# Two groups of block one's input projections taken in 512-column products, with their halves copied out by ScalarE and added by GpSimd

## The reference, cut to what matters

```
h = rmsnorm(x, mix_pre_norm[l])
u = h @ w_in[l]
u_z, u_xbc, u_dt, u_ly, u_lx, u_g = jnp.split(u, list(IN_SPLITS), axis=-1)
y_a = ssd_mixer(u_z, u_xbc, u_dt, ...)
y_b = rglru_mixer(u_ly, u_lx, ...)            # gate = gelu(u_ly); return h * gate
g = jax.nn.sigmoid(u_g.reshape(b, s, N_BRANCHES, D_MODEL) + gate_b[l])
merged = g[:, :, 0, :] * (y_a @ w_proj_ssm[l]) + g[:, :, 1, :] * (y_b @ w_proj_lru[l])
x = x + rmsnorm(merged @ w_out[l], mix_post_norm[l])
```

## Time and profile before

| | |
|---|---|
| time before, median of 3 runs | 838.07 us (837.78 to 838.09) |
| the profiled execution's own time | 837.62 us |
| its span, first to last instruction | 835.8 us |
| PE busy | 825.4 us (99% of the span) |
| DVE busy | 638.2 us (76%) |
| ACT busy | 502.9 us (60%) |
| POOL busy | 74.0 us (9%) |
| mean granted TensorE clock | 0.998 |

### The profile page before, as it was taken

One profiled execution on the slowest core, in us unless ns is written; L12 is line 12 of the kernel. 1 busy time (PEld: TensorE's weight loads), 2 busy tenths in 40 slices (PEclk: granted clock), 3 DMA queues, 4 the chain that ended last, 5 costly groups with the idle time before them and its releaser, 6 DMA issues. The chain is left out here.

```text
span 835.8 us, 14603 instructions
## 1 busy us (share of the span) xinstructions
PE 825.4 (99%) x5782; PEld 741.8 (89%) x5782; DVE 638.2 (76%) x1146; ACT 502.9 (60%) x828; POOL 74.0 (9%) x71
## 2 busy tenths in 40 slices
PE   8999999999999999999999999999999999999996
PEld 6999999999989988888888789899899888888885
DVE  6887987998968778788878869777664566776765
ACT  6575778665267755556566878853544454555453
POOL 0200001101020111111111200040000020001000
PEclk9999999999999999999999999999999999999999
DMA  8657443467464746554655465574333333465541
GB/s 306 235 180 285 155 150 106 150 215 284 138 220 152 250 155 209 193 184 171 208 194 189 137 213 194 144 258 155 123 106 126 136 117 103 151 206 182 191 151 51
DMA packets 42812, 147.81 MB, mean 177 GB/s; under 512 B 6876, under 2 KB 7672, under 8 KB 42232
## 3 DMA queue, kind: packets, MB, share of 16 engines
q1 hardware_dynamic: 42600, 146.75, 52.5%
q10 hardware_dynamic: 144, 0.13, 0.0%
HBM read 145.79 MB, written 1.08 MB: 176 GB/s over the span
## 5 line engine op out<-in xcount | busy, mean ns | idle before, releaser
L2042 DVE TENSOR_TENSOR t_wl<-t_raw,t_wh 128x1024 fp32r<-128x1024 f32 x256 | 312.1, 1229 | 78.8 <-ACT t_wh L1464 77.9
L1464 ACT ACTIVATE t_wh<-t_raw 128x1024 fp32r<-128x1024 f32 x256 | 268.0, 1055 | 92.1 <-PE bank L674 89.7
L674 PE MATMUL bank<-t_hx,t_wh 128*128 128x256 f32 (+1 forms) x1968 | 298.5, 302 | 0.3 <-ACT t_hx L1475 0.3
L674 PEld LDWEIGHTS bank<-t_hx,t_wh 128*128 128x128 f32 x1968 | 263.6, 191 | 13.3 <-issue 1.1
L674 PE MATMUL bank<-t_hx,t_wl 128*128 128x256 f32 x1136 | 160.1, 283 | 0.0
L674 PEld LDWEIGHTS bank<-t_hx,t_wl 128*128 128x128 f32 x1136 | 149.2, 191 | 3.0
L674 PE MATMUL bank<-t_wh,t_hx 128*128 128x512 f32 x440 | 122.3, 400 | 0.0
L674 PE MATMUL bank<-t_wh,t_br 128*128 128x512 f32 x384 | 103.9, 392 | 0.0
L674 PEld LDWEIGHTS bank<-t_wh,t_hx 128*128 128x128 f32 x440 | 80.8, 188 | 17.5 <-ACT t_wh L1464 0.9
L674 PEld LDWEIGHTS bank<-t_wh,t_br 128*128 128x128 f32 x384 | 70.9, 188 | 14.1 <-issue 0.2
L674 PE MATMUL bank<-t_wl,t_hx 128*128 128x512 f32 x220 | 67.7, 390 | 0.0
(11 more groups left out here) (152 smaller groups left out, 685.4 us busy)
## 6 DMA issues: line engine op xcount, KB each, us to landing
t_raw<-in_ws SPq DMA_DIRECT2D x258, 512.0 KB, 4.2
t_br<-decay SPq DMA_DIRECT2D x1, 2048.0 KB, 8.8
t_arena<-in_post SPq DMA_DIRECT2D x3, 512.0 KB, 5.1
t_x<-in_xin SPq DMA_DIRECT2D x2, 512.0 KB, 4.5
t_bd<-in_bd SPq DMA_DIRECT2D x1, 1024.0 KB, 6.3
t_x<-in_xtok SPq DMA_DIRECT2D x1, 1024.0 KB, 6.5
t_arena<-in_mem SPq DMA_DIRECT2D x1, 1024.0 KB, 8.6
out<-t_x SPq DMA_DIRECT2D x3, 256.0 KB, 2.3
```

What stands on the lines that cost most here:

```text
L674: return e.matmul(o, l, r, start=st, stop=sp, skip_group_check=True)
L1464: e.activation(high(q), RAW[q % NR][:, :], ACT.Copy, bias=0.0, scale=1.0).then_inc(*hi.now(q))
L2042: e.tensor_tensor(low(q), RAW[q % NR][:, :], high(q).bitcast(F), SUB).then_inc(*lo.now(q))
```

## The change

`ly0` to `ly3` and `g4` to `g7` go through `chunk_apart`. Each of their 16 units gets a PSUM bank of its own (banks 0 to 2 in turn; before, one bank per chunk). After each unit ACT copies the bank's 512 columns to a half of `PX` (`PARTS`), which is double-buffered by the unit's place in the chunk, and POOL adds the two parts (128x256) into `LY` or `GG`. For `g4` to `g7` ACT then applies Tanh in place on `GG`, once POOL's second addition of the chunk is done. DVE's program is the same, instruction for instruction.

```diff
+BESIDE = [f"ly{i}" for i in range(4)] + [f"g{i}" for i in range(4, 8)]
...
+        elif name in BESIDE:
+            for i in range(2):
+                n = (n + 1) % 3
+                bank[name, i] = n
...
+        PARTS = [PX[:, 512 * i:512 * i + 512].rearrange("p (w t) -> p w t", w=2) for i in range(2)]
...
+        g_both = tally("parts_added")
...
+                if name[0] in BESIDE:
+                    return a_ev.of("beside", *name)
...
             for i in range(4):
-                chunk(f"ly{i}", Hh, Hl)
+                chunk_apart(f"ly{i}")
             for i in range(4, 8):
-                chunk(f"g{i}", Hh, Hl)
+                chunk_apart(f"g{i}")
...
-                    e.wait_ge(*a_ev.of(f"ly{q}"))
+                    e.wait_ge(*g_both.of(f"ly{q}", 1))
...
+            def parts_out(name):
+                for j in range(2):
+                    q = walk.unit()
+                    e.wait_ge(*unit.of(q))
+                    n = BESIDE.index(name)
+                    if n > 0:
+                        e.wait_ge(*g_both.of(BESIDE[n - 1], j))
+                    act(PARTS[j], two(BANK[name, j]), ACT.Copy).then_inc(*a_ev.now("beside", name, j))
+                    walk.tick()
...
             def gates(i):
-                walk.cols(f"g{i}", i == 0)
-                chunk_done(f"g{i}")
+                name = f"g{i}"
+                if name in BESIDE:
+                    parts_out(name)
+                    e.wait_ge(*g_both.of(name, 1))
+                else:
+                    walk.cols(name, i == 0)
+                    chunk_done(name)
...
-                    m = act(GG[:, k, :], half(BANK[f"g{i}"], j), ACT.Tanh, bias=hgb[:, k:k + 1], scale=0.5)
+                    src = GG[:, k, :] if name in BESIDE else half(BANK[name], j)
+                    m = act(GG[:, k, :], src, ACT.Tanh, bias=hgb[:, k:k + 1], scale=0.5)
...
             for i in range(4):
-                walk.cols(f"ly{i}")
-                chunk_done(f"ly{i}")
-                act(LY[:, 2 * i:2 * i + 2, :], two(BANK[f"ly{i}"]), ACT.Copy).then_inc(*a_ev.now(f"ly{i}"))
+                parts_out(f"ly{i}")
...
+            def added(name, dst, k):
+                for j in range(2):
+                    walk.unit()
+                    e.wait_ge(*a_ev.of("beside", name, j))
+                    tt(dst[:, k + j, :], PARTS[j][:, 0, :], PARTS[j][:, 1, :], ADD).then_inc(*g_both.now(name, j))
+                    walk.tick()
...
             for i in range(4):
-                walk.cols(f"ly{i}")
+                added(f"ly{i}", LY, 2 * i)
...
             for i in range(4, 8):
-                walk.cols(f"g{i}")
+                added(f"g{i}", GG, 2 * i)
```

## The result

The changed kernel takes 849.88 us (median of 4 runs, 849.46 to 850.55); the kernel before, on the same chip, 838.08 (837.78 to 838.31). The ratio is 1.0143, 95% interval 1.0131 to 1.0155: slower by 11.8 us, where 7.8 were forecast. The profiled execution took 849.46 us, against 837.62 before.

The account below looks back on a forecast made before the run. PE, 99% busy, bounds the kernel, with DVE's queue level with it up to `YBl(3)`; +1.0 and +6.9 there make PE 7.8 us later: 837.62 + 7.8 = 845.4, forecast 845.9 as median, range 841.0 to 850.5 (8 in 10).

Parts of the forecast that it names:

- C: Rival: ACT also becomes a bound, its waits for POOL delaying splits and copies; 2 to 4 us more, 849; 0.25 with D.
- D: Rival: the clock falls while PE waits in unit 52, 1.5 or 2.5 us lost, 848; 0.25 with C, the smaller part.
- the chain on DVE ends level with PE's: From 143.5 to 183.8 us DVE's queue has no slack; PE has 0.1 us to spare at `YBl(3)`, so DVE's delay is the kernel's.
- Term 1: Unit 37's copy ahead of ACT's Exp delays the split of unit 41, so DVE's queue starts 1.0 us later.
- Term 2: POOL's 13 additions of units 38 to 50 each lengthen DVE's queue by 0.53 us: +6.9 us (0 to 9.4).
- The upper bound, the whole 0.72 us: The most one POOL addition could cost DVE: the whole length of such an operation on POOL, 0.72 us.
- PE's 1.3 us: Sixteen units at 2.80 instead of 2.88 us save PE 1.3 us, forecast to be lost in its wait for DVE.
- The other waits of PE: Earlier bank reuse costed at nothing; waits at low weights and `y_pair`s lie inside the delay at `pl0`.
- the four multiplies: POOL's multiplies, only spread: three stood in DVE's way before, at 1.1 us each, and three will afterwards; no term.
- Rival A: Half of POOL's additions cost DVE nothing, falling while it waits for something else; 842.5 us; chance 0.17.
- Rival B: Neither term delays DVE at `YBl(3)`, so PE's faster products show their 1.3 us; 836.8 us; chance 0.06.
- the stages behind: Sign to look for in the profile after: the stages behind the changed stretch each take as long as before.

Follow-up runs that it names:

- e3: The changed kernel with 24 and 9 useless products on PE ahead of its waits for `YBl(2)` and `YBl(3)`; 845.82 us, ratio 1.0095.
- e1: The changed kernel with POOL's 16 additions replaced by zero fills that read nothing, sums left out; 840.47 us, ratio 1.0040.
- e5: The changed kernel with POOL's additions cut to 128x128, the other half of each sum set to zero; 845.78 us, ratio 1.0098.
- e4: The changed kernel with ACT's copy of unit 37 moved behind the Exp and the square root; 849.57 us, ratio 1.0139.
- e2: The kernel before plus only sixteen 128x256 additions of zeros on POOL, into a buffer nobody reads; 846.18 us, ratio 1.0097.
- e6: The changed kernel's 512-column products alone: ACT takes only the high halves, no POOL additions, low parts' share left out; 838.13 us, ratio 1.0000.
- e9: The kernel of e6 with the recurrence's four 128x512 multiplies on DVE instead of POOL; 837.71 us, ratio 0.9997.
- e7: The changed kernel's products, with DVE reducing each bank's two parts out of PSUM, no ACT copies or POOL additions; 852.13 us, ratio 1.0162.
- e8: The change made for g4 to g7 only, ly0 to ly3 as in the kernel before; 845.80 us, ratio 1.0089.

## Why the forecast was right, and by what it fell short

The direction, and a time within 841.0 to 850.5, were forecast; the main sum, 845.9, was not met. By my own bands, 849.88 us lies above 847.8, where I had put 0.25 for C and D, and C, to which I gave the larger part, did not happen. D brought it there, at a price that I had put too low. The range held with 0.6 us to spare, because it had room for C as well as for D, and that part is luck. DVE's delay came out at 7.9 us for 7.8, by the mechanism of the sum.

**That the chain on DVE ends level with PE's, so that its delay is the kernel's.** Right. `YBl(3)` ended at 191.70 for 191.7 forecast, released PE there, and nothing was given back behind. Where the clock was kept up (e3), the kernel took 845.82 us for 845.9.

**Term 1, the copy of unit 37 ahead of the Exp, +1.0.** Right: 144.54 for 143.53, with the executions in step ahead of it. Counted from unit 40's split it is 7.17 us for 6.19, and 7.17 again in e1, e3 and e5, which keep ACT's order. e4 adds what I hadn't seen: most of the microsecond isn't free to be won back, since POOL then works beside DVE and not ahead of it.

**Term 2, 13 x 0.53 = 6.9.** The sum is right, in part by luck, by two small errors that cancel: it was fourteen additions at 0.49, because with DVE so late unit 51's came ahead of `YBl(3)`, and because one of them fell on a gating that reads PSUM. In e2, where four did, the mean was 0.41. That turns are the cause stands on e1 (POOL writes only: gone), e2 (additions alone: there) and e5 (half the size: half the turn). The upper bound, the whole 0.72 us, is out as a mean.

**PE's 1.3 us, lost in the wait.** Right: PE's units were 2.80 us apart wherever it didn't wait (starts at 171.34, 174.14, 176.93), and it stood the longer at `YBl(2)`. Whether they would be lost without the additions as well isn't shown: e6 and e9 were no faster than the kernel before, but with 0.99 and 0.61 us of bank waits of their own in the way, and with a scatter of nearly the size in question. What the gain would be in a kernel with both obstacles removed stays open.

**The other waits of PE, at nothing, and the four multiplies, no term.** Right in sum: PE waited 1.94 us for a low split and 0.31 and 0.2 for decays on the way, inside DVE's delay; the multiplies and casts cost DVE what they had cost before, within 0.2 us by my estimate from the lengthened operations.

**Rival D is what the forecast falls short by.** The sum has no term for the clock, and that is its one wrong step. I had the fall as a mechanism, beside the sum, and mis-sized its price: "PE does 3 us of work at half speed, 1.5 us lost, or 2.5 if it takes 5 us to return". The clock stayed low for 10.25 us, and that cost 9.22 - 5.29 = 3.9 us in the trace and 4.06 in the medians (e3). Having it only as a rival was the second half of the mistake: the forecast itself had PE stand several microseconds in one place, and the earlier trace rows showed a fall within some 3 us of standing still. How long it would last stands in none of the rows. Of the signs that I had named, the stages behind, "each as long as before", is the one that failed. The sum closes: slice 6 of unit 52 at 191.75 for 183.90 is 7.85, with 3.9 it is 11.8, and the profiled executions differ by 849.46 - 837.62 = 11.84.

**Rival A** (turns cost half) is out: DVE had no gap to hide a turn in. **Rival B** is out for the changed kernel, where DVE was 7.9 us late. Its 836.8 us did not appear in e6 either, where DVE had no delay, but e6's own bank waits stood in the way, so that part of it stays untested. **Rival C** did not happen in the changed kernel, where ACT waited 1.8 us in all for POOL; it did in e5 and, with DVE in POOL's place, in e7.

The Trainium skill, in "SBUF — State Buffer", section "Who interferes with whom", had the kind of operations right. Of its sentence that whoever issues first holds the port pair for the whole instruction the runs show less: 0.49 us on the mean for DVE, and at most 0.57, from additions that take 0.72 us on POOL while DVE reads PSUM.

## What to carry to other kernels

Look, in the stretch that a change touches, for the second engine that is busy all the time, even if over the whole kernel it has a quarter to spare; work handed to a third engine is then not free when that engine reads SBUF beside it, and its price is so many operations times one turn, read from a place where both already work. When such a sum makes TensorE stand for microseconds in one place, price the clock with it: here 4 us on top of 8, and 4 again on top of the 4 of half the change. A saving on the engine that looks full is worth nothing before the one that ends level with it has been made shorter.

## What the hardware showed that I had not expected

- **The length of a turn goes with POOL's columns, not with DVE's operation.** A DVE operation that reads SBUF is lengthened by 0.26 to 0.28 us beside a 128x128 addition (e5), by 0.40 to 0.57 beside a 128x256 one (the changed kernel and e8), by 1.1 beside a 128x512 one. Where DVE was reading PSUM at the moment, only 0.15 to 0.26 were left of a 128x256 turn (e2, and 0.17 at 172.73 in the changed kernel).
- **POOL can be kept out as well.** A 128x128 addition took 2.69 us (e5, at 174.66) while DVE's operations followed one another without a gap.
- **A wait of 3.2 us was followed by 10.25 us at 1.2 GHz, though PE had work for nearly all of them** (45 products in 9.5 busy us). The clock went from 2.4 to 1.2 GHz only about the end of the wait: in the changed kernel at 190.3, where the wait ended at 190.01, in e8 at 186.5, where it ended at 186.97; and 24 products of no use in that wait kept it at 2.4. Shorter waits did it too: e5, with waits of 1.81 and 2.33 us, had 6.8 us at the low level from 186.7 on, and the wait of 1.94 us in the changed kernel was followed by 3.4 us of it.
- **Writing on POOL costs DVE nothing** (e1: sixteen 128x256 fills of 0.31 to 0.46 us, fourteen of them inside DVE's queue, no DVE operation longer beside them).
